# Inversion's matrices in rooms of their own with early triangle products, and a third unit of the values' projection ahead of the first attention's near products

## The reference

```python
def token_mixer(u, ...):
    p = (u @ w_in).astype(jnp.float32)          # pool | hgrn | rwkv | gla columns
    o_h = chunked_gated_linear_attention(q, 1 - f, v, log f)      # "hgrn"
    y_hgrn = rms_norm_2(o_h, hgrn_norm) * sigmoid(hg)
    o_r = rwkv7_scan(r, decay, k, v, kk, a)     # S = S diag(w) - (S kk)(kk a)^T + v k^T
    y_rwkv = (group_norm(o_r) + bonus) * g_r
    o_g = chunked_gated_linear_attention(q, k, v, log_a)          # "gla"
    y_gla = rms(o_g) * gla_norm * silu(gg)
    return concat([y_pool, y_hgrn, y_rwkv, y_gla]) @ w_out
```

## Time and profile before

| what | value |
|---|---|
| median of three runs | 1682.84 us (1681.21 to 1686.25) |
| the profiled execution's own time | 1683.53 us |
| its span, first to last instruction | 1681.4 us |
| PE busy | 1638.9 us, 97% |
| DVE, ACT, POOL busy | 862.1, 667.8, 127.2 us |
| mean granted clock of PE | 0.986 |

### The profile page before, as it was taken

One profiled execution on the slowest core, in us unless ns is written; L12 is line 12 of the kernel. 1 busy time (PEld: TensorE's weight loads), 2 busy tenths in 40 slices (PEclk: granted clock), 3 DMA queues, 4 the chain that ended last, 5 costly groups with the idle time before them and its releaser, 6 DMA issues.

```text
span 1681.4 us, 23771 instructions
## 1 busy us (share of the span) xinstructions
PE 1638.9 (97%) x9520; PEld 1328.4 (79%) x9520; DVE 862.1 (51%) x1170; ACT 667.8 (40%) x1018; POOL 127.2 (8%) x127
## 2 busy tenths in 40 slices
PE   9999999999999999999999999997999999999997
PEld 6877778877777888888888878785877888888886
DVE  6733445552444565444433478668557554444333
ACT  6145565314656433333323355346433433333221
POOL 0001001000100110000000310000410200000000
PEclk9999999999999999999999999998899999999998
DMA  5412212341221323322333322220012233222331
GB/s 181 154 63 76 88 51 88 113 126 63 71 81 51 101 76 112 100 91 98 91 96 102 135 81 65 63 63 1 14 36 82 88 101 100 94 94 84 102 103 50
DMA packets 40749, 144.13 MB, mean 86 GB/s; under 512 B 4816, under 2 KB 4832, under 8 KB 40256
## 3 DMA queue, kind: packets, MB, share of 16 engines
q1 hardware_dynamic: 37296, 131.61, 24.6%
q0 software_dynamic: 2192, 8.87, 1.6%
q10 hardware_dynamic: 1152, 2.14, 0.4%
HBM read 140.50 MB, written 2.10 MB: 85 GB/s over the span
## 4 chain that ended last, share of the span: by engine, by line
PE 88%; DVE 7%; ACT 3%; issue 1%; DMA 0%; DVEq 0%; SPq 0%; ACTq 0%
PE bank L500 26%; PE bank L502 25%; PE bank L501 25%; PE bank L482 2%; PE bank L1044 2%; PE bank L488 2%; PE bank L865 1%; PE bank L667 1%; PE bank L731 1%; PE bank L710 1%; DVE sb_w_low L1260 1%; ACT sb_w_high L2033 1%; PE bank L589 0%; DMA sb_x<-xT 0%; DVE sb_near L1674 0%
## 5 line engine op out<-in xcount | busy, mean ns | idle before, releaser
L1260 DVE TENSOR_TENSOR sb_w_low<-sb_raw,sb_w_high 128x1024 fp32r<-128x1024 f32 (+1 forms) x253 | 312.1, 1234 | 365.5 <-ACT sb_w_high L2033 359.0
L500 PE MATMUL bank<-sb_xg_high,sb_w_high 128*128 128x512 f32 x1176 | 465.4, 396 | 1.4 <-DVE sb_w_low L1260 1.4
L502 PE MATMUL bank<-sb_xg_high,sb_w_low 128*128 128x512 f32 x1176 | 458.7, 390 | 0.0
L501 PE MATMUL bank<-sb_xg_low,sb_w_high 128*128 128x512 f32 x1176 | 458.6, 390 | 0.0
L2033 ACT ACTIVATE sb_w_high<-sb_raw 128x1024 fp32r<-128x1024 f32 (+1 forms) x253 | 263.2, 1040 | 347.4 <-PE bank L502 323.2
L500 PEld LDWEIGHTS bank<-sb_xg_high,sb_w_high 128*128 128x128 f32 x1176 | 221.1, 188 | 63.3 <-issue 15.8
L502 PEld LDWEIGHTS bank<-sb_xg_high,sb_w_low 128*128 128x128 f32 x1176 | 221.2, 188 | 46.8
L501 PEld LDWEIGHTS bank<-sb_xg_low,sb_w_high 128*128 128x128 f32 x1176 | 221.3, 188 | 44.6 <-issue 0.2
L502 PE MATMUL bank<-sb_h_high,sb_w_low 128*128 128x512 f32 x352 | 136.9, 389 | 0.0
L500 PE MATMUL bank<-sb_h_high,sb_w_high 128*128 128x512 f32 x352 | 136.9, 389 | 0.0
L501 PE MATMUL bank<-sb_h_low,sb_w_high 128*128 128x512 f32 x352 | 136.9, 389 | 0.0
(11 more groups left out here) (344 smaller groups left out, 1965.9 us busy)
## 6 DMA issues: line engine op xcount, KB each, us to landing
sb_raw<-w_ffn_in SPq DMA_DIRECT2D x88, 512.0 KB, 3.5
sb_raw<-w_ffn_out SPq DMA_DIRECT2D x32, 512.0 KB, 3.5
sb_raw<-w_tok SPq DMA_DIRECT2D x24, 512.0 KB, 3.6
sb_raw<-w_mix_f SPq DMA_DIRECT2D x18, 512.0 KB, 3.5
sb_raw<-w_rot SPq DMA_DIRECT2D x16, 512.0 KB, 3.6
sb_raw<-w_qk SPq DMA_DIRECT2D x16, 512.0 KB, 3.4
sb_raw<-w_out SPq DMA_DIRECT2D x16, 512.0 KB, 3.4
sb_raw<-w_ffn_out SPq DMA_DIRECT2D x16, 384.0 KB, 3.1
```

The costliest lines, as they stand in the source:

```text
L500: e.matmul(out, w[0], v[0], start=first, stop=False)
L501: e.matmul(out, w[0], v[1], start=False, stop=False)
L502: return e.matmul(out, w[1], v[0], start=False, stop=last)
L1260: e.tensor_tensor(out, a, b, op).then_inc(*v.up(*signal))
```

## The change

Rooms: X and XT of a head lie side by side, two heads in each of gla's two factor buffers (whose order is reversed, so that heads 0 and 1 lie in the buffer read first); AT lies beside Pm, CT beside A_ak, Gv in rwkv's output, W1 and the offset in the room of the far scores. ACT presets heads 0 and 1 after level 128 and heads 2 and 3 after level 256. PE makes AT and X of heads 0 and 1 ahead of gla's values, waiting for bI alone, and of heads 2 and 3 behind them. DVE takes the triangles of heads 0 and 1 between the two halves of key work, those of 2 and 3 after kI. Bonus sums and operand turns move into level 2, the turns of gla's values into level 4, and gla's normalisation is cut into pieces that follow the updates of levels 4, 8 and 16. gla's gate is one Silu on ACT; POOL's multiply goes. The fillers of hgrn move one level ahead. The order in which the weight units are loaded follows that of their use.

```diff
-    values, projections = mixer_group(1), mixer_tiles(*range(2, 10))
-    order += values[0:3] + [projections[0], values[3]] + projections[1:]
+    order += mixer_group(1) + mixer_tiles(*range(2, 10))
...
-        m.gate_sigmoid = self.square.rearrange("p f (a b) -> p (f a) b", b=G)
...
+        m.E2 = [r.room("E", 2, SEQ) for _ in range(2)][::-1]
...
+        two = lambda room: (room[:, :, 0:TT * CHUNK], room[:, :, TT * CHUNK:2 * TT * CHUNK])
+        m.Pm, m.AT = two(r.room("Pm_AT", 4, TT * P))
+        m.A_ak, m.CT = two(r.room("A_ak_CT", 2, TT * P))
+        m.X, m.XT = two(region(factors_at, kept_at).room("X_XT", 4, TT * P))
+        m.Gv = flat(m.y_tok["rwkv"]).rearrange("p (h n) -> p h n", h=4)
+        r = region(far_at, kept_at)
+        m.W1, m.offset = r.room("W1", TT, G), r.room("offset", TT, G)
...
+        operand_of = {"AT": "bI", "X": "bI", "A_ak": "kI", "M_rk": "rE", "M_rb": "rE"}
+
+        def gram(what, two, left, right):
+            out = [take((what, h), {"AT": ("XT made", 2, h), "X": ("X made", 2, h)}.get(what, (what, h))) for h in two]
+            p.wait_ge(*of(operand_of[what]))
...
                 if before_last and n == len(ORDER) - 1:
                     before_last()
+                    keep_busy(1)
+                scores(n)
+                if before_last and ORDER[n] == 64:
                     keep_busy(2)
-                scores(n)
             if name == "gla":
                 fill(len(ORDER))
+                gram("AT", HEAD_PAIRS[0], m.bI, m.kkE)
+                gram("X", HEAD_PAIRS[0], m.kkE, m.bI)
             values()
...
                 pool_outputs()
+                next(values_h)
             else:
-                next(values_h if n < 3 else others if n < 8 else values_g)
+                next(values_h if n < 2 else others if n < 7 else values_g)
...
-            if n < 2:
+            if n == 0:
                 next(values_g)
-                next(projections)
-            elif n < 6:
+            if n < 6:
...
+            p.wait_ge(*of("kI"))
...
-        bonus = take(("bonus",), ("bonus",))
-        held.add(bonus)
-        for two in HEAD_PAIRS:
-            gram("AT", two, m.bI, m.kkE)
-            if not two[0]:
-                bonus_sums(0)
-                bonus_sums(1)
-            gram("X", two, m.kkE, m.bI)
-            if not two[0]:
-                bonus_sums(2)
-                bonus_sums(3)
-            for t in two:
-                turn_operands(t)
-            if not two[0]:
-                turn_values("gla", 0)
-                turn_values("gla", 1)
-        held.discard(bonus)
+        def bonus_sums():
+            i = take(("bonus",), ("bonus",))
+            p.wait_ge(*of("bonus products"))
+            for t in range(TT):
+                for f in range(2):
+                    at = 4 * t + 2 * f
+                    group(banks[i][:, at:at + 2], [(m.sigma[:, f, blk(t)], mem.table("same_head")[:, 0:P:64])],
+                          "bonus in")
+
+        gram("AT", HEAD_PAIRS[1], m.bI, m.kkE)
+        gram("X", HEAD_PAIRS[1], m.kkE, m.bI)
...
+            if size == 2:
+                bonus_sums()
             for h in HEADS:
                 if h + 2 < 4:
                     updates(h)
                     product(h + 2)
                 else:
+                    if size == 2:
+                        turn_operands(2 * h - 4)
+                        turn_operands(2 * h - 3)
+                    elif size == 4:
+                        turn_values("gla", h - 2)
...
                 reduce(ms, split(squares), "mean square", name)
+                yield
                 v.wait_ge(*of("root", name))
                 recip(ms, ms, *STEP)
                 tt(split(y), split(y), ms.unsqueeze(2).to_broadcast([P, n_norms, width]), ALU.mult, *STEP)
+                yield
                 tt(y, y, v2[:, :, G:], ALU.mult, "y made", name)
+                yield
 
...
-            stt(m.bI, m.bI, -1.0, eI, ALU.mult, ALU.mult, *STEP)
+            stt(m.bI, m.bI, -1.0, eI, ALU.mult, ALU.mult, "bI")
...
-            tt(m.kI, rk, eI, ALU.mult, *STEP)
-            tt(m.rE, rr, m.eB, ALU.mult, "rE")
+                stt(m.sigma[:, f, :], rr[:, f, :], mem.col("rwkv_r_k", f), rk[:, f, :], ALU.mult, ALU.mult,
+                    "bonus products")
+                if f == 0:
+                    first_triangles(m, 0)
+                    first_triangles(m, 1)
+            tt(m.kI, rk, eI, ALU.mult, "kI")
...
+    def first_triangles(m, h):
+        masked("AT", m.AT[:, h, :], h, mem.table("before"))
+        for name, what, ap, mask in (("XT", "AT", m.XT, mem.chunk_pairs(1)), ("X", "X", m.X, mem.table("pairs_ts"))):
+            v.wait_ge(*of(what + " product", h))
+            v.wait_ge(*of(name + " preset", h))
+            e.copy_predicated(chunks(ap[:, h, :]), over_tiles(mask).bitcast(I32),
+                              chunks(bank(what, h)[:, 0:TT * CHUNK])).then_inc(*v.up(name + " made", 2, h))
...
+        first_triangles(m, 2)
+        first_triangles(m, 3)
+        tt(m.rE, m.mixed[:, 0:2, :], m.eB, ALU.mult, "rE")
+        finishing = finish_gla()
...
+            if size > 2:
+                next(finishing, None)
...
+                if name == "gla" and ORDER[n] == 128:
+                    preset((0, 1), n)
             if name == "gla":
                 fill(len(ORDER))
+                bend_gate("gla")
+                preset((2, 3), len(ORDER) - 1)
             for f in range(2):
...
+        def preset(two, level):
+            a.wait_ge(*of("factors read", "gla", level))
+            for name, out in (("XT", m.XT), ("X", m.X)):
+                for h in two:
+                    act(chunks(out[:, h, :]), over_tiles(mem.table("chunk_ident")), name + " preset", h)
...
-            if name == "hgrn":
-                act(gate, gate, "gate bent", name, func=ACT.Sigmoid)
-            else:
-                act(m.gate_sigmoid, gate, "gate sigmoid", func=ACT.Sigmoid)
+            act(gate, gate, "gate bent", name, func=ACT.Sigmoid if name == "hgrn" else ACT.Silu)
...
-            if size in (2, 4):
+            if size in (4, 8):
                 use()
+            if size == 4:
+                land_mixed("gla")
+                finish_gla()
...
-        gate = m.operands["gla"][3][:, :, G:]
-        g.wait_ge(*of("gate sigmoid"))
-        tt(gate, gate, m.gate_sigmoid, ALU.mult, "gate bent", "gla")
...
-            g.wait_ge(*of("y made", "gla"))
+            g.wait_ge(*of("values", "gla", 1))
```

117 lines of the change are left out of this document (37 added, 80 removed).

## The result

The changed kernel takes 1690.12 us (median of 20 runs, 1682.30 to 1694.15), the kernel before 1682.64 (20 runs, 1680.95 to 1686.25). The ratio is 1.0037, with a 95% interval of 1.0027 to 1.0048. The forecast was 1677.2, with a range up to 1682.5.

The account below looks back on a forecast made before the run. PE was taken to bound the kernel, with DVE the bound at the mixer stage's end. Terms 1.8-0.7-1.5-10.4+0.9+2.3+1.6+0.4 = -5.6 gave 1677.2 us against the median of 1682.8; range 1672.5 to 1682.5.

Parts of the forecast that it names:

- +1.8 us: First attention: PE's stall ahead of the third unit grows from 2.2 to 4.05 us; bounds +0.5 and +3.5.
- every level keeps its cover: First attention: with the remaining fillers one level ahead, each level still has covering work; no cost counted.
- -0.7: Second attention: the fourth near bank's 0.72 us wait for the first rwkv projection goes, the values' banks being free.
- so nothing: Second attention: first level's scores lose one of two cover units, but DVE has factors some 2 us ahead; no cost.
- both scans at 1.2 us: Sign at sb_cum: with POOL's multiply gone, the 2703 ns scan takes 1225, shortening the chain to bI by 1.5 us.
- 21.4 us from bI to level 4: End of bI to level 4's products: forecast 21.45 us against 31.9, so -10.4, if DVE keeps up.
- the waits of 1.5 and 2.6 us: Level 2's first use of tokB waits 1.5 us; level 8 waits for ACT's landed product, +2.3 (1.5 to 3.3).
- The tail's terms: Mixer stage's end, scans through inversion: -1.5 -10.4 +0.9 +2.3 +1.6 +0.4, forecast -6.7 us.
- Rival 2: DVE or ACT bounds level 2 (+1.5), and clock falls at bonus sums and third unit (+1.8): 1680.5; 0.25 with rival 4.
- Rival 3: PE falls to 1.2 GHz in level 2, from bonus sums on, and stays there through the inversion: 1686; chance 0.08.
- Rival 1: No half-speed stretch behind the level 8 wait (-1.6) or at the third unit (-1.6): 1674; chance 0.17.
- The 0.06 for slower: Whole kernel: chance of a time above 1687.9 us, from the worse half of rival 3 and causes not thought of.

Follow-up runs that it names:

- norms later: Changed kernel with hgrn's first scores in the near products' banks, plus the sums of key squares one projection later: 1683.2 us, ratio 1.0003 to the kernel before.

## Why the prediction was wrong

**The step that failed** is the first attention: "PE stands still for 4.05 us instead of 2.2: +1.8 us", with the bounds +0.5 and +3.5, and with it "The rest of the fillers moves one level ahead and every level keeps its cover" and, for the second attention, "-0.7" and "so nothing". Together +1.1 us. The runs show +9.8 on the new inversion. From the pool's products to gla's near products the kernel before takes 96.66 us and the changed one 104.16 and 110.16, with one unit of some 5.4 us more: +2.1 in the first profile and +8.1 in the second, against the forecast +1.8. From there to the low-rank product it is +3.1 in both, against -0.7. In detail:

- The wait of 4.1 us was right, and its direct cost too: 1.9 us more idle time.
- I took the low clock behind it as equal to today's. In the first profile that holds: 0.79 over 7.1 us are 1.5 us lost, against 0.53 over 3.5, 1.6 us, before. In the second it doesn't: 0.54 over 7.1 us, 3.3 us lost, still within my upper bound of +3.5. Filling the wait gives back 3 to 5 us of the median.
- "Every level keeps its cover" looked at the number of units and not at the banks. The values' last unit moved directly ahead of scores that take its banks: 1.9 us idle, and 5 to 7 us with the low clock behind it (about 5 us lost from 1012 to 1040 in the second profile). For this the sum had no term and the range no room.
- "So nothing" for gla looked at whether the next factors were ready. They were. What moved was ACT's order, the landings ahead of the root, and a lead of DVE over PE that was spent three levels later: 0.35 us for w_low, 1.78 for the key squares, 1.67 of low clock, less the 0.72 of the earlier trace rows that did go. These come to the 3.1 us. That the low clock comes from the wait is not shown ("norms later" has it without the wait).

**What was right.** The idle time of 4 us at 991 to 995, no wait at gla's near products, both scans at 1.2 us, the first triangle product 0.15 us behind bI, 21.4 us from bI to level 4, the waits of 1.5 and 2.6 us (forecast 1.5 and 2.3), some 3.4 us of low clock behind the latter. The tail's terms sum to -6.7 and both profiles of the changed kernel show -6.4, against the one profile of the kernel before (89.1; the old inversion behind the moved unit took 90.7). Level 4 began 6.6 us earlier on the clock of the trace and not 11 to 13, since it started 5.4 late.

**The tail's term was mis-sized as a median.** Alone, the inversion gives 1.2 us, not 6.7: in its profile the tail is 3 us longer than in the changed kernel's, by low clock at level 2 and behind. Rival 2 had named this place, and priced it at 1.8 together with the first attention's. With dummies in the waits, which shorten none of the work, the same inversion is 6.2 us under the kernel before (0.9963). That speaks for clock as most of what was missing. But the comparison rests on one group of 11 runs without dummies, and the dummies gave 1.5 us where a third one stood ahead of level 128.

**The rivals.** Rival 3 put the loss into the inversion; the side was right and the place wrong. Rival 1 (the clock holds) didn't come in the changed kernel; with the wait filled, the clock held at the third unit (1.00). The 0.06 for slower was far too small: each stall that I added was priced as idle time plus at most one low stretch, and I let no rival stand for several levels losing the clock together.

## What to carry to other kernels

In this kernel a wait of PE cost its length and often low clock behind it, and the second part varied from execution to execution. A single profile may show the cheapest case, so look at the mean clock of several runs of the same kernel before trusting the difference of two spans. Between kernels the mean clock doesn't do: low clock in idle time is free, and on work it is not. Before moving a long-held unit, write out which banks the next taker gets and who empties them, and whose landings change places in the program of the engine that lands. Where a wait can't be removed, dummy products that fit into it are cheap to try: here they gave some 2 to 5 us.

## What was not expected of the hardware

- The same program runs between 1682.3 and 1694.2 us, along with PE's mean granted clock (0.992 to 0.985). The two executions with a trace (1682.3 and 1689.3) have the same waits.
- 1.9 us of idle time, removed, gave 5 to 7 us; 4.1 us of idle time, filled and not removed, gave 3 to 5.
- The low clock also comes without a wait directly ahead of it: at 1175 to 1185, with PE busy all the time, in the sums two columns wide and the products beside them; the last wait had ended at 1167.6, and the clock had been at 1.00 for 10 us since. In the changed kernel's profiles the same instructions run at 1.00. At 1135 to 1140 of "norms later" it is 0.66, with PE busy since 1122.
